# Expert rows added by DMA onto one residual row per token, instead of two stored rows per token that are combined at the end

## The chip, the cores and the metric

The kernel runs on one core of one Trainium2 chip. The metric is the device time of one execution in microseconds (us), the median of three runs. TensorE (PE) multiplies matrices, VectorE (DVE), ScalarE (ACT) and GpSimd (POOL) work on rows, SyncE (SP) only issues transfers, and 16 DMA engines carry out the transfers of all queues.

## The reference

One layer of a streaming encoder on 64 sample tokens, 16 meta tokens and 1024 prompt tokens (1104 tokens of 1024 float32 each), then a final RMSNorm. The part that the change touches is the mixture of experts: each token goes to two of 32 experts, and the two outputs, each times its gate, are added to the residual row.

```python
h = x + mix.astype(x.dtype)                       # residual row of the token
hn = rmsnorm(h, norm_ffn)
gates = p_g * top_v / sum(top_v)                  # two gates per token
expert(x) = (silu(x @ w_eg[e]) * (x @ w_eu[e])) @ w_ed[e]
h = h + gate_0 * expert_0(hn) + gate_1 * expert_1(hn)
y = rmsnorm(h, norm_final)                        # meta rows dropped
```

## The kernel before, in words

Nothing is scheduled by a planner: each engine has its own program, written out in order, and the engines meet at semaphores. A wait holds up everything behind it on its engine.

**Front stage** (to about 500 us). 1152 rows (1104 tokens and 48 padding rows) are worked in 9 tiles of 128 rows. For each tile PE projects, mixes and multiplies by the output weights; DVE adds the result to the residual tile `h_all[:, j, :]` in `back_h` (semaphore `h_added`), which stays in SBUF to the end. ACT normalises the tile and stores it to DRAM as `hn_rows`, **twice**: once in the rows of pick 0 and once in those of pick 1 (L624). The router gives each row two experts and two gates (`gate_all`, `back_weights`), and `back_rank` its place among the 96 slots of an expert. `mark` (L1332) is a small product on PE which turns one-hot matrices into the table `idx_i`: slot by expert, the row of `hn_rows`. An empty slot holds an index out of bounds, and the DMA skips it.

**Expert stage** (about 502 to 1053 us). The experts come one after another, in pairs of buffers b = 0, 1. For expert e POOL gathers up to 96 rows (`gather`, L481), PE transposes them, multiplies by the gate weights (L1412), by the up weights (L1412 again, semaphore `pe_u2`) and by the down weights (L1423, L1429, semaphore `pe_d`). DVE and ACT make the SiLU between. ACT copies the result from PSUM to `ye[b]` (L697, L699), and POOL scatters `ye[b]` to DRAM (`scatter`, L492). Each of the 2208 picks has a row of its own in `pick_rows`, so no scatter meets another. SP loads the weights, 3 x 2 MB per expert: `w_eg` (L394) as soon as the gate product of expert e-2 has freed the buffer, `w_eu` (L399) after its up product, `w_ed` (L402) after its down product.

**Extra slots.** An expert with more than 96 rows would get further blocks, in code that is there and was not entered with these inputs (n_x = 0).

**Last stage** (1053 us to the end). SP waits for the last scatters and loads `pick_rows` back, two tiles y1 and y2 for each of the 9 token tiles (L438, 18 DMAs). For each tile DVE does two operations in `combine` (L1142: y1*gate0 + h; L1144: + y2*gate1), ACT takes the sum of squares and the reciprocal root (L729 to L731), DVE normalises (L1150), and SP stores the tile (L442, L444).

Of the kernel before, what the change touches and what calls it, by code (L numbers as in the profile page):

```python
# [21 lines left out]
F32 = mybir.dt.float32  # L22
# [6 lines left out]
P = 128  # L29
# [35 lines left out]
PICK_ROWS = PICKS * TILES * P  # L65
# [17 lines left out]
           ("iota_block", BLOCK), ("iota_e", NE), ("first_g", GROUPS), ("first_e", PER_GROUP), ("pick", PICKS),  # L83
# [9 lines left out]
def constants():  # L93
# [16 lines left out]
    put("pick", p + TILES * P * np.arange(PICKS)[None, :] - NO_ROW)  # L110
# [45 lines left out]
def build(nc, x_all, state_pool, state_gla, norm_mix, w_in, w_gate_up, b_gate, w_pool, pool_scale, gla_norm, w_out,  # L156
          norm_ffn, w_router, b_router, w_eg, w_eu, w_ed, norm_final, const,
          y_prompt, y_sample, pool_prompt, gla_prompt, pool_sample, gla_sample):
    hn_dram = nc.dram_tensor("hn_rows", (PICK_ROWS, D), F32, kind="Internal").ap()
    y_dram = nc.dram_tensor("pick_rows", (PICK_ROWS, D), F32, kind="Internal").ap()  # L160

    with ExitStack() as ctx:
# [93 lines left out]
        M_tok = sb("M_tok", [P, PICKS, NE])  # L256
# [5 lines left out]
        token = sb("token", [P, PICKS])  # L262
# [4 lines left out]
        idx_f = sb("idx_f", [BLOCK, NE])  # L267
# [30 lines left out]
        idx_xf = sb("idx_xf", [BLOCK, EXTRA])  # L298
# [6 lines left out]
        def lot(n):  # L305
            return arena[:, n * D:(n + 1) * D]
        y1 = [lot(2 * i) for i in range(TILES)]
        y2 = [lot(2 * i + 1) for i in range(TILES)]
# [4 lines left out]
            w_out_in w_out_scaled hn_stored  # L313
            pe_xT pe_z pe_gate pe_qk pe_u pe_r pe_v pe_pool pe_kT pe_scores pe_kv pe_o pe_ones pe_wout pe_hT
            pe_router pe_rank pe_idx pe_hist_T pe_small_T
# [4 lines left out]
            u_kept s_sample_ready pool_out_ready outs_stored idx_ready slots_ready  # L320
            parted dve_front dve_back dve_back_o dve_rank dve_once dve_moe dve_fin act_front act_back act_once act_fin history_kept pool_steps
            pe_eT pe_g pe_u2 pe_d sig_ready hid_ready eT_ready ye_ready row_idx_ready
            x_tab_dve x_tab_pe x_idx_ready x_w x_rows x_pe x_dve x_act x_stored x_pool pick_idx_ready
            fin_ready frstd_ready g_fin_in""").split()
# [15 lines left out]
        TABLE_STEPS = 10  # L340
# [6 lines left out]
        def _(sp):  # L347
# [85 lines left out]
            for b in range(2):  # L433
                sp.wait_ge(ye_stored[b], 16 * (NE // 2))
            for i in range(TILES):
                for k, y in ((0, y1[i]), (1, y2[i])):
                    at_row = (k * TILES + i) * P
                    sp.dma_start(y[0:OUT_ROWS[i], :], y_dram[at_row:at_row + OUT_ROWS[i], :]).then_inc(y_in[i], 16)  # L438
            for i in range(TILES):
                sp.wait_ge(out_ready[i], 1)  # L440
                if i == 0:
                    sp.dma_start(y_sample, y2[i][0:SAMPLE, :]).then_inc(s["outs_stored"], 16)  # L442
                else:
                    sp.dma_start(y_prompt[(i - 1) * P:i * P, :], y2[i]).then_inc(s["outs_stored"], 16)  # L444
# [4 lines left out]
        def _(pool):  # L449
# [25 lines left out]
            pool.wait_ge(s["hn_stored"], 16 * PICKS * TILES)  # L475

            def gather(t, b):
# [4 lines left out]
                                             bounds_check=PICK_ROWS - 1, oob_is_err=False).then_inc(rows_in[b], 16)  # L482
# [17 lines left out]
            gather(1, 1)  # L500
            scatter(0, 0, first=True)
# [13 lines left out]
            pool.wait_ge(s["pe_eT"], NE)  # L515
            with pool.If(n_x > 0):
                with pool.Fori(0, EXTRA) as n:
                    with pool.If(n < n_x):
# [3 lines left out]
                                                     bounds_check=PICK_ROWS - 1, oob_is_err=False).then_inc(s["x_rows"], 16)  # L522
# [212 lines left out]
        def _(dve):  # L735
# [204 lines left out]
            def body(i, first=False, last=False, second=False, third=False):  # L940
# [6 lines left out]
                if ranking:  # L947
                    rank.begin(i - 2)
                    back_rank(i - 2, third)
# [586 lines left out]
```

## Time and profile before

| | us |
|---|---|
| median of 3 runs (1103.26 to 1104.48) | 1104.26 |
| the profiled execution | 1103.76 |
| its span, first to last instruction | 1101.9 |
| PE busy | 1012.4 (92%) |
| DVE / ACT / POOL busy | 417.4 / 240.8 / 104.8 |
| granted TensorE clock, mean | 0.966 |

The page cuts the span into 40 slices of 27.5 us. Its row PE is at 9 from the second slice to the 38th with one dip at the change of stages, and its row DMA is at 9 only in the expert stage and at the start. The last two slices hold no product. In the rows below a start is counted in us from the start of the span. SPq and POOLq are DMAs issued by that engine. "DMA to landing" is the time from the issue of a DMA to the completion of its data.

### The profile page before, as it was taken

How to read it: one execution, taken by the hardware profiler on the slowest of the kernel's cores; microseconds unless marked ns; L12 is line 12 of the kernel's file. 1: busy time of each engine (PE TensorE's matmuls, PEld its weight loads, DVE VectorE, ACT ScalarE, POOL GpSimd, SP SyncE). 2: the span in 40 equal slices, each digit the busy share in tenths (PEclk: the TensorE clock that was granted, in tenths of full speed). 3: DMA queues.
4: the chain of work that ended last, by engine and by line, in shares of the span. 5: the costliest groups of instructions: out<-in, count | busy, mean ns of one | idle time of the engine just before them, and what ended most of it. 6: DMA issues, size and time to landing. Idle time of an engine off the chain costs nothing.

```text
span 1101.9 us, 32850 instructions
## 1 busy us (share of the span) xinstructions
PE 1012.4 (92%) x14634; PEld 822.7 (75%) x14634; DVE 417.4 (38%) x909; ACT 240.8 (22%) x506; POOL 104.8 (10%) x172
## 2 busy tenths in 40 slices
PE   5999999999999999875999999999999999999920
PEld 5786777768685958435888898898888888988910
DVE  1434443535253535243432332332322323323338
ACT  2352232323332321210111111011111111111123
POOL 0110101010110101001111011011110110110000
PEclk9999999999999999986999999999999999999965
DMA  8900000000000000384999999999999999999557
GB/s 272 402 5 39 1 39 0 38 0 38 4 34 38 0 38 1 152 322 173 373 375 393 405 399 411 408 404 401 398 410 403 395 409 404 397 405 401 215 214 300
DMA packets 50850, 262.17 MB, mean 238 GB/s; under 512 B 8205, under 2 KB 10701, under 8 KB 42618
## 3 DMA queue, kind: packets, MB, share of 16 engines
q1 hardware_dynamic: 41050, 234.05, 53.8%
q0 software_dynamic: 7168, 18.10, 4.8%
q10 hardware_dynamic: 2592, 9.44, 2.1%
q8 instruction: 31, 0.51, 0.2%
q14 instruction: 9, 0.07, 0.0%
HBM read 241.84 MB, written 26.80 MB: 244 GB/s over the span
## 4 chain that ended last, share of the span: by engine, by line
PE 91%; DVE 5%; DMA 2%; issue 1%; ACT 1%; SPq 0%; ACTq 0%; DVEq 0%; POOLq 0%; POOL 0%
PE bank L1412 31%; PE bank L1178 18%; PE bank L1303 11%; PE bank L1423 10%; PE bank L1230 6%; PE bank L1429 5%; PE bank L1166 4%; DVE arena L1144 1%; DVE arena L1142 1%; PE bank L1279 1%; DMA arena<-in_w_in 1%; DVE arena L1150 1%; PE bank L1237 1%; PE bank L1296 1%; PE bank L1290 1%
## 5 line engine op out<-in xcount | busy, mean ns | idle before, releaser
L1178 PE MATMUL bank<-xnT,arena 128*128 128x128 f32 x1728 | 201.5, 278 | 4.9 <-DMA arena<-in_w_in 3.5
L1178 PEld LDWEIGHTS bank<-xnT,arena 128*128 128x128 f32 x1728 | 197.1, 193 | 7.6 <-DMA arena<-in_w_in 4.0
L1412 PEld LDWEIGHTS bank<-xnT,arena 128*64 128x64 f32 x4096 | 171.8, 138 | 8.9 <-issue 8.9
L1412 PE MATMUL bank<-xnT,arena 128*64 128x96 f32 x4096 | 175.0, 248 | 2.2 <-issue 2.2
L1412 PEld LDWEIGHTS bank<-hnT,arena 128*64 128x64 f32 x4096 | 169.6, 137 | 7.4 <-issue 7.4
L1412 PE MATMUL bank<-hnT,arena 128*64 128x96 f32 x4096 | 172.8, 246 | 0.6 <-issue 0.6
L1026 DVE TENSOR_SCALAR mixT<-mixT 128x384 f32<-128x384 f32 x32 | 11.5, 360 | 324.0 <-ACT mixT L692 324.0
L1303 PE MATMUL bank<-arena,mixT 128*128 128x512 f32 x288 | 127.8, 602 | 3.0 <-DVE mixT L859 3.0
L1303 PEld LDWEIGHTS bank<-arena,mixT 128*128 128x128 f32 x288 | 54.9, 193 | 69.4 <-issue 65.7
L1423 PE MATMUL bank<-arena,silu_r 128*32 128x384 f32 x768 | 86.0, 487 | 0.5 <-issue 0.5
L1429 PE MATMUL bank<-arena,silu_r 128*32 128x256 f32 x384 | 85.9, 380 | 0.0
L1429 PE MATMUL bank<-arena,osq 128*32 128x256 f32 x384 | 85.9, 380 | 0.0
L1423 PE MATMUL bank<-arena,osq 128*32 128x384 f32 x768 | 85.8, 488 | 0.0
L1027 DVE RECIPROCAL mixT<-mixT 128x384 f32<-128x384 f32 x32 | 81.7, 2553 | 1.1
L1230 PE MATMUL bank<-arena,xnT 128*128 128x512 f32 x144 | 64.6, 592 | 0.0
L1429 PEld LDWEIGHTS bank<-arena,osq 128*32 128x32 f32 x384 | 40.9, 110 | 15.0
L697 ACT ACTIVATE hs<-bank 96x384 f32<-96x384 f32 x32 | 13.8, 482 | 174.3 <-PE bank L1429 174.3
L697 ACT ACTIVATE kz_v<-bank 96x384 f32<-96x384 f32 x32 | 13.8, 482 | 173.5 <-PE bank L1429 173.5
L1429 PEld LDWEIGHTS bank<-arena,silu_r 128*32 128x32 f32 x384 | 40.9, 110 | 14.4
L460 POOL TENSOR_TENSOR window_work<-window_work 128x568 f32<-128x568 f32 x9 | 10.2, 1132 | 401.4 <-ACT window_work L586 401.4
L1230 PEld LDWEIGHTS bank<-arena,xnT 128*128 128x128 f32 x144 | 26.1, 190 | 26.3 <-issue 26.3
L692 ACT ACTIVATE mixT<-bank 128x384 f32<-128x384 f32 x32 | 15.7, 490 | 127.0 <-PE bank L1412 127.0
(193 smaller groups left out, 934.8 us busy)
## 6 DMA issues: line engine op xcount, KB each, us to landing
arena<-in_w_eg SPq DMA_DIRECT2D x32, 2048.0 KB
arena<-in_w_eu SPq DMA_DIRECT2D x32, 2048.0 KB
arena<-in_w_ed SPq DMA_DIRECT2D x32, 2048.0 KB, 15.4
hn_rows<-hs ACTq DMA_DIRECT2D x18, 512.0 KB, 3.5
arena<-pick_rows SPq DMA_DIRECT2D x16, 512.0 KB, 10.1
arena<-in_w_in SPq DMA_DIRECT2D x3, 2048.0 KB, 14.5
arena<-in_w_out SPq DMA_DIRECT2D x1, 4096.0 KB, 25.7
out_y_prompt<-arena SPq DMA_DIRECT2D x8, 512.0 KB, 3.5
```

The source lines that it names most:

```text
L692: A(sig[:, 0:NH], bank[2 + b][:, 0:NH], ACT.Exp, scale=-1.0).then_inc(s["sig_ready"], 1)
L697: A(ye[b][:, half * OWN:(half + 1) * OWN], bank[6 + half][0:BLOCK, 0:OWN], ACT.Copy).then_inc(s["ye_ready"], 1)
L1026: moe.then(V.tensor_scalar(gs[:, 0:NH], sig[:, 0:NH], 1.0, None, ALU.add))
L1027: moe.then(V.reciprocal(gs[:, 0:NH], gs[:, 0:NH]))
L1142: final.then(V.scalar_tensor_tensor(out=y1[i][0:r, :], in0=y1[i][0:r, :], scalar=gate_all[0:r, i, 0:1], in1=h_all[0:r, i, :], op0=ALU.mult ...
L1166: return nc.tensor.transpose(out, src, ident[0:n, 0:n])
L1178: last = mm(out, w_in_sb[:, k, a:b], xnT[:, k, :], start=k == 0, stop=k == KD - 1)
L1230: last = mm(bank[6][:, :], xnT[:, k, :], w_in_sb[:, k, V0:R0], start=k == 0, stop=k == KD - 1)
L1303: done = mm(bank[n][:, :], mixT[:, k, :], w_out_sb[:, k, n * 512:(n + 1) * 512], start=k == 0, stop=k == KD - 1)
L1412: last = mm(out[q * SW:(q + 1) * SW, n * BLOCK:(n + 1) * BLOCK], w[:, k, m * P + q * SW:m * P + (q + 1) * SW], rowsT[b][:, k, :], start=k ...
L1423: last = mm(bank[6 + half][g * TG:(g + 1) * TG, 0:OWN], tokens(k, g), wd[b][:, k, half * OWN:(half + 1) * OWN], start=k == 0, stop=k == KF ...
L1429: return mm(bank[n][TGS * TG:P, c:c + REST], tokens(k, g), wd[b][:, k, 2 * OWN:D], start=k == 0 and c == 0, stop=k == KF - 1, skip_group_c ...
```

## The change

1. `hn_rows` has one row per token, and ACT stores each normalised tile once.
2. A new DRAM tensor `sum_rows` has one row per token. SP stores each tile of the residual there as soon as it is added (`store_h`): eight before the first expert weights are loaded, the ninth behind the weights of experts 0 and 1.
3. The front stage builds, next to the table of indices, a table `gate_of_slot`: slot by expert, the gate. `mark` has 64 columns in place of 32, DVE gets `mark_gates`, and `back_weights` moves ahead of `back_rank`. For the last tile the gate half is done by PE inside expert 0, between its gate and its up product.
4. ACT multiplies by the gate while it copies the result from PSUM (`scale=gate` in `put_rows`).
5. The scatter adds (`compute_op=ALU.add`) onto `sum_rows`. As two experts may meet in one row, each scatter now waits until the one before has landed, and the first one for all residual tiles.
6. The last stage loads one row per token, 9 DMAs in place of 18, into `h_all`. `combine` is gone: ACT takes the squares of what was loaded, DVE normalises it.

```diff
-    hn_dram = nc.dram_tensor("hn_rows", (PICK_ROWS, D), F32, kind="Internal").ap()
-    y_dram = nc.dram_tensor("pick_rows", (PICK_ROWS, D), F32, kind="Internal").ap()
+    hn_dram = nc.dram_tensor("hn_rows", (ROWS, D), F32, kind="Internal").ap()
+    sum_dram = nc.dram_tensor("sum_rows", (ROWS, D), F32, kind="Internal").ap()
...
+            def store_h(j):
+                sp.wait_ge(s["h_added"], j + 1)
+                sp.dma_start(sum_dram[j * P:(j + 1) * P, :], h_all[:, j, :]).then_inc(s["h_stored"], 16)
+
+            for j in range(TILES - 1):
+                store_h(j)
             sp.wait_ge(s["pe_v"], TILES)
             load_weights(0, 0)
             load_weights(0, 1)
+            store_h(TILES - 1)
...
+            sp.wait_ge(s["h_stored"], 16 * TILES)
             for i in range(TILES):
-                for k, y in ((0, y1[i]), (1, y2[i])):
-                    at_row = (k * TILES + i) * P
-                    sp.dma_start(y[0:OUT_ROWS[i], :], y_dram[at_row:at_row + OUT_ROWS[i], :]).then_inc(y_in[i], 16)
+                sp.dma_start(h_all[0:OUT_ROWS[i], i, :], sum_dram[i * P:i * P + OUT_ROWS[i], :]).then_inc(y_in[i], 16)
...
             def scatter(t, b, first=False):
                 e = 2 * t + b
+                if not (first and b == 0):
+                    wait_parted(pool, ye_stored[1 - b], 16 * (t + b), s["parted"])
...
-                nc.gpsimd.indirect_dma_start(y_dram, bass.IndirectOffsetOnAxis(ap=pick_idx[b][:, :], axis=0), ye[b], None,
-                                             bounds_check=PICK_ROWS - 1, oob_is_err=False).then_inc(ye_stored[b], 16)
+                nc.gpsimd.indirect_dma_start(sum_dram, bass.IndirectOffsetOnAxis(ap=pick_idx[b][:, :], axis=0), ye[b], None, compute_op=ALU.add,
+                                             bounds_check=ROWS - 1, oob_is_err=False).then_inc(ye_stored[b], 16)
...
-                for k in range(PICKS):
-                    act.dma_start(hn_dram[bass.ds(k * TILES * P + j * P, P), :], hs[:, :, :].rearrange("p k n -> p (k n)")).then_inc(s["hn_stored"], 16)
+                act.dma_start(hn_dram[bass.ds(j * P, P), :], hs[:, :, :].rearrange("p k n -> p (k n)")).then_inc(s["hn_stored"], 16)
...
+            def put_rows(out, gate, step):
+                for half in range(2):
+                    A(out[:, half * OWN:(half + 1) * OWN], bank[6 + half][0:BLOCK, 0:OWN], ACT.Copy, scale=gate[:, :]).then_inc(step, 1)
...
-                act.wait_ge(s["fin_ready"], i + 1)
+                act.wait_ge(y_in[i], 16)
...
+            def mark_gates(j):
+                gates = gate_all[:, bass.ds(j, 1), :].rearrange("p a k -> p (a k)")
+                Mk = M[:, :, :, :].rearrange("p k g e -> p k (g e)")
+                return V.tensor_tensor(M_tab[:, :, NE:], Mk, gates.unsqueeze(2).to_broadcast([P, PICKS, NE]), ALU.mult)
...
-            for i in range(TILES):
-                combine(i)
-                if i:
-                    normalize(i - 1)
-            normalize(TILES - 1)
+            for i in range(TILES):
+                normalize(i)
...
+                if isinstance(t, int) and e == 0:
+                    pe.wait_ge(s["gmarks_ready"], 1)
+                    mark(NE, 2 * NE).then_inc(s["pe_gates"], 1)
                 pe.wait_ge(u_in[b], 16 * t + 16)
```

**The order on POOL** in the loop over the experts, for buffer 0: `rows_idx` and `pick_idx` hold the indices of the gather and of the scatter. Before:

```order
L481 DMA window_work<-hn_rows,rows_idx 96x1024 [waits row_idx_ready]
L121 ISA
L489 ISA [waits ye_stored0]
L489 COPY pick_idx<-idx_i 96x1
L121 REGISTER_ALU
L121 REGISTER_ALU [waits pick_idx_ready]
L492 DMA pick_rows<-kz_v,pick_idx 2304x1024 [waits ye_ready]
```

And with the change:

```order
L490 DMA window_work<-hn_rows,rows_idx 96x1024 [waits row_idx_ready]
L121 ISA
L500 ISA [waits ye_stored1,ye_stored0]
L500 COPY pick_idx<-idx_i 96x1
L121 REGISTER_ALU
L121 REGISTER_ALU [waits pick_idx_ready]
L503 DMA sum_rows<-kz_v,pick_idx 1152x1024 [waits ye_ready]
```

The wait for the other buffer's scatter is new; the next gather stands behind it.

**The order on DVE** in the last stage (first tile has 64 rows, the others 128; `fss` is the reciprocal root). Before, the first eight of 26 rows (27 operations):

```order
L1142 SCALAR_TENSOR_TENSOR arena<-arena,gate_all,h_all 64x1024
L1144 SCALAR_TENSOR_TENSOR arena<-arena,gate_all 64x1024
L1142 SCALAR_TENSOR_TENSOR arena<-arena,gate_all,h_all 128x1024
L1144 SCALAR_TENSOR_TENSOR arena<-arena,gate_all 128x1024
L1150 SCALAR_TENSOR_TENSOR arena<-arena,fss 64x1024
L1142 SCALAR_TENSOR_TENSOR arena<-arena,gate_all,h_all 128x1024
L1144 SCALAR_TENSOR_TENSOR arena<-arena,gate_all 128x1024
L1150 SCALAR_TENSOR_TENSOR arena<-arena,fss 128x1024
```

And with the change, the whole stage:

```order
L1172 SCALAR_TENSOR_TENSOR arena<-h_all,fss,arena 64x1024
L1172 SCALAR_TENSOR_TENSOR arena<-h_all,fss,arena 128x1024 x8
```

Eighteen of 27 operations are gone, and what is left waits for ACT, which waits for the load.

## Rows read from the trace of the kernel before

**Rows 1.** The page's 40 slices of the span, tenths of busy time and GB/s.
```profile
PE   5999999999999999875999999999999999999920
DMA  8900000000000000384999999999999999999557
GB/s 272 402 5 39 1 39 0 38 0 38 4 34 38 0 38 1 152 322 173 373 375 393 405 399 411 408 404 401 398 410 403 395 409 404 397 405 401 215 214 300
```

**Rows 2.** Expert stage: busy PE, PEld, DVE, ACT, POOL, clock, DMA share, GB/s.
```profile
660.00:760.00 100.00, 100.00 (x2001) 87.44 (x2001) 30.69 (x42) 14.91 (x36) 14.19 (x24) 1.00 1.02 405
```

**Rows 3.** Timeline of SP: last two loads of down weights (start, duration).
```profile
1002.82 0.38 SPq L402 DMA_DIRECT2D arena<-in_w_ed  x1
...
1019.66 0.38 SPq L402 DMA_DIRECT2D arena<-in_w_ed  x1
```

**Rows 4.** Line L402, landing of its 5 loads issued from 500 to 600 us.
```profile
DMA to landing us min/median/max: 10.8/12.5/14.9
```

**Rows 5.** Line L402, landing of the load issued at 1002.82 us.
```profile
DMA to landing us min/median/max: 18.1/18.1/18.1
```

**Rows 6.** Timeline of PE: first down products of experts 30 and 31.
```profile
1030.92 0.52 PE L1423 MATMUL bank<-arena,osq 128*32 128x384 f32 x3
...
1047.52 0.52 PE L1423 MATMUL bank<-arena,silu_r 128*32 128x384 f32 x3 [0.51 <-issue]
```

**Rows 7.** The page's DMA queues: packets, MB, share of 16 engines' span.
```profile
q1 hardware_dynamic: 41050, 234.05, 53.8%
q0 software_dynamic: 7168, 18.10, 4.8%
```

**Rows 8.** Timeline of POOL: the scatters of experts 28 and 31, the last one.
```profile
1005.79 0.94 POOL L492 DMA_INDIRECT pick_rows<-kz_v,pick_idx  x1 [13.76 <-ACT kz_v L699]
...
1055.86 0.92 POOL L492 DMA_INDIRECT pick_rows<-hs,pick_idx  x1 [15.38 <-ACT hs L699]
```

**Rows 9.** Line L492, all 32 scatters.
```profile
DMA to landing us min/median/max: 3.3/7.1/9.5
```

**Rows 10.** Groups of the last stage by form: busy, mean ns, idle before.
```profile
L1144 DVE SCALAR_TENSOR_TENSOR arena<-arena,gate_all 128x1024 f32<-128x1024 f32 x8 | 10.3, 1285 | 0.3
L1150 DVE SCALAR_TENSOR_TENSOR arena<-arena,fss 128x1024 f32<-128x1024 f32 x8 | 10.2, 1280 | 0.6 <-ACT fss L731 0.6
L1142 DVE SCALAR_TENSOR_TENSOR arena<-arena,gate_all,h_all 128x1024 f32<-128x1024 f32 x8 | 10.2, 1277 | 0.0
L729 ACT ACTIVATE arena<-arena 128x1024 f32<-128x1024 f32 x8 | 8.5, 1057 | 14.8 <-DVE arena L1144 14.8
L730 ACT ACTIVATE fss<-fss,eps 128x1 f32<-128x1 f32 x8 | 2.4, 294 | 0.3
L731 ACT ACTIVATE fss<-fss 128x1 f32<-128x1 f32 x8 | 1.6, 203 | 0.3
L729 ACT ACTIVATION_READ_ACCUMULATOR arena<-arena 128x1 f32 x8 | 1.5, 186 | 0.0
```

**Rows 11.** Timeline of the last stage: SP's loads, DVE's first and last operation.
```profile
1059.23 11.49 SPq L438 DMA_DIRECT2D arena<-pick_rows  x18
1064.68 1.28 DVE L1142 SCALAR_TENSOR_TENSOR arena<-arena,gate_all,h_all 64x1024 f32<-64x1024 f32 x1 [16.02 <-DMA arena<-pick_rows]
...
1097.55 1.28 DVE L1150 SCALAR_TENSOR_TENSOR arena<-arena,fss 128x1024 f32<-128x1024 f32 x1 [0.58 <-ACT fss L731]
```

**Rows 12.** Line L438, landing of the 18 loads.
```profile
DMA to landing us min/median/max: 4.1/9.4/15.1
```

**Rows 13.** Line L444, landing of the 8 stores of the output.
```profile
DMA to landing us min/median/max: 2.6/3.5/11.9
```

**Rows 14.** A stretch of the last stage, columns as in rows 2.
```profile
1065.00:1080.00 15.00, 0.00 (x0) 0.00 (x0) 14.82 (x13) 6.59 (x16) 0.00 (x0) 0.50 1.03 412
```

**Rows 15.** Timeline of a front tile: DVE's wait before the ranks, PE's `mark`.
```profile
267.57 0.19 DVE L921 TENSOR_TENSOR R<-bank,counts 128x32 f32<-128x32 f32 x1 [2.02 <-PE bank L1327]
...
274.61 0.45 PE L1332 MATMUL bank<-M_tok,at_rank 128*96 128x32 f32 x4
```

More of the change, by code:

```diff
@@ L306, in lot @@
             return arena[:, n * D:(n + 1) * D]
-        y1 = [lot(2 * i) for i in range(TILES)]
-        y2 = [lot(2 * i + 1) for i in range(TILES)]
+        squares = [lot(2 * i) for i in range(TILES)]
+        y_out = [lot(2 * i + 1) for i in range(TILES)]
         g_fin = lot(2 * TILES)
@@ L515, in _ @@
             pool.wait_ge(s["pe_eT"], NE)
+            for b in range(2):
+                pool.wait_ge(ye_stored[b], 16 * (NE // 2))
             with pool.If(n_x > 0):
@@ L684, in _ @@
             back_router(TILES - 1)
+            def put_rows(out, gate, step):
+                for half in range(2):
+                    A(out[:, half * OWN:(half + 1) * OWN], bank[6 + half][0:BLOCK, 0:OWN], ACT.Copy, scale=gate[:, :]).then_inc(step, 1)
+                for g, (n, c) in enumerate(REST_AT):
+                    own = slice(g * TG, (g + 1) * TG)
+                    A(out[own, 2 * OWN:D], bank[n][BLOCK:P, c:c + REST], ACT.Copy, scale=gate[own, :]).then_inc(step, 1)
             def expert(t, b, first=False):
@@ L695, in expert @@
                     act.wait_ge(ye_stored[b], 16 * t)
-                for half in range(2):
-                    A(ye[b][:, half * OWN:(half + 1) * OWN], bank[6 + half][0:BLOCK, 0:OWN], ACT.Copy).then_inc(s["ye_ready"], 1)
-                for g, (n, c) in enumerate(REST_AT):
-                    A(ye[b][g * TG:(g + 1) * TG, 2 * OWN:D], bank[n][BLOCK:P, c:c + REST], ACT.Copy).then_inc(s["ye_ready"], 1)
-            act.wait_ge(s["hn_stored"], 16 * PICKS * TILES)
+                if first and b == 0:
+                    act.wait_ge(s["gates_ready"], 1)
+                put_rows(ye[b], gate_of_slot[:, bass.ds(e, 1)], s["ye_ready"])
+            act.wait_ge(s["hn_stored"], 16 * TILES)
             expert(0, 0, True)
@@ L932, in back_rank @@
                     rank(V.tensor_scalar(at_rank[:, k, :], con("iota_block"), rk[:, k:k + 1], None, ALU.is_equal))
-                V.tensor_tensor(M_tok[:, :, :], Mk, token[:, :].unsqueeze(2).to_broadcast([P, PICKS, NE]), ALU.mult).then_inc(s["onehot_ready"], 1)
+                if not last:
+                    rank(mark_gates(j))
+                V.tensor_scalar(M_tab[:, :, 0:NE], Mk, token[:, 0:1], None, ALU.mult).then_inc(s["onehot_ready"], 1)
             def back_idx(j):
@@ L948, in body @@
                     rank.begin(i - 2)
+                    back_weights(i - 2)
                     back_rank(i - 2, third)
@@ L992, in _ @@
             rank.begin(j - 1)
+            back_weights(j - 1)
             back_rank(j - 1)
@@ L1004, in _ @@
             rank.begin(j)
-            back_rank(j)
+            back_rank(j, last=True)
             dve.wait_ge(s["idx_added"], TILES)
             dve.wait_ge(s["pe_idx"], TILES)
-            V.tensor_tensor(idx_i[:, :], idx_f[:, :], bank[7][0:BLOCK, 192:192 + NE], ALU.add).then_inc(s["idx_ready"], 1)
+            V.tensor_tensor(idx_i[:, :], idx_f, bank[7][0:BLOCK, 192:192 + NE], ALU.add).then_inc(s["idx_ready"], 1)
             back_weights(j)
+            mark_gates(j).then_inc(s["gmarks_ready"], 1)
             moe = Steps(dve, s["dve_moe"])
@@ L1391, in _ @@
             ranks(j)
-            mark(j)
+            pe.wait_ge(s["onehot_ready"], j + 1)
+            mark(0, NE).then_inc(s["pe_idx"], 1)
             STRIPS = 2
@@ L1452, in expert @@
                 pe.wait_ge(s["hid_ready"], 2 * e + 2)
-                if not (isinstance(t, int) and e == 0):
+                if isinstance(t, int) and e == 0:
+                    pe.wait_ge(s["gates_ready"], 1)
+                else:
                     pe.wait_ge(s["ye_ready"], YE_STEPS * e)
```

111 lines of the change are left out of this document (54 added, 57 removed).

## The prediction

> **What bounds the kernel now.** I read the 40 slices first [rows 1]. The reader is to see that PE is at 9 almost from start to end, that DMA is at 9 only in the expert stage, and that two slices at the end hold no product at all. Then I took one stretch of the expert stage [rows 2]: in 100 us PE is busy for 100.00 and the DMA share is 1.02 at 405 GB/s. So two resources are full at once, at a granted clock of 1.00, the higher of its two levels (2.4 GHz). PE sets the pace, one expert in 1019.66 - 1002.82 = 16.84 us [rows 3]. Per expert the DMA engines move 6.29 MB of weights (32 such sets), and 2208/32 = 69 picked rows of 4096 B in and again out, 0.57 MB: 6.86 MB in 16.84 us are 407 GB/s, the 405 of the row.
>
> That the DMA engines have nothing to spare shows in the landing of the down weights. The first ones take 10.8 to 14.9 us [rows 4], one near the end 18.1 us [rows 5]: a queue that grows under a constant demand. It does no harm yet. The weights of expert 30 land at 1002.82 + 18.1 = 1020.9 and are used at 1030.9, so 10.0 us are left; for expert 31 the use is at 1047.5 [rows 3, 5, 6]. These 10 us are the only cover that the change has for more DMA work.
>
> The last stage is bound by DVE: 27 operations back to back from 1064.68 to 1098.8 [rows 11], 1.28 us each [rows 10], with almost no idle time before them, while ACT waited 14.8 us for them. After DVE's last operation 3 us remain for the last store [rows 13] (2.6 at least), and the span ends at 1101.9.
>
> **The last stage.** Eighteen operations of `combine` go, 10.3 + 10.2 us for 16 of them [rows 10] and 2.6 for the first tile's two. What is late next? Three chains have to be worked out from the issue of the last scatter, 1055.86 [rows 8]. It landed in at least 3.3 us [rows 9], which gives the loads' issue at 1059.23 [rows 11]. An add has to read its target first; I give it 1 us more, so the loads are issued at 1060.2.
> - ACT: the first tile lands 4.1 us later [rows 12], at 1064.3. ACT takes 1.057 + 0.186 + 0.294 + 0.203 = 1.74 us per tile [rows 10], nine tiles 15.7: 1080.0. DVE's 1.28 and a store of 2.6 to 3.5 follow [rows 10, 13]: 1084.
> - DMA: 4.46 MB in and 4.46 MB out at 412 GB/s [rows 14] are 21.7 us. They start about 1.5 us after the issue and need about 1.5 us to complete the last: 1085.
> - DVE: nine operations of 1.28, hidden behind ACT.
>
> The loads go first in the same queue, so the stores can't start before them, and DMA is the bound: the end is at 1085 in place of 1101.9, **16.9 us earlier**. The DMA bytes of this stage fall from 13.4 to 8.9 MB.
>
> **The expert stage.** Scatters stay 32, with the same 69 rows each, but each row is now read from DRAM, added and written. The trace has no adding DMA. From below it costs nothing more: if the read of the target passes beside the writes of other rows. Less than nothing is excluded, as the same rows are still read from SBUF and written to DRAM. From above, if each row had to finish before the next could start, 69/16 = 4.3 rows per engine would each hold it for a large part of the 3.3 us of the fastest scatter [rows 9], say 2.4: 10 us per expert. Between them lie two rows. The loads' queue q1 took 53.8% of 1101.9 us for 234.05 MB, which is 0.166 us of one engine per 4096 B; q0, with gathers and scatters, 4.8% for 18.10 MB, 0.192 us per row with its overhead [rows 7]. One more read of 4096 B, at the rate of q1, is 4.3 x 0.166 = **0.72 us per expert**; as costly as a whole second row of q0 it would be 0.83. I take 0.72, as the added part is a read without a descriptor for a new row; the row nearest to it is q1's.
>
> What of it is paid: when the weights of expert 30 are needed, scatters 0 to 28 have been issued (28 at 1005.79 [rows 8]). 29 x 0.72 = 20.8 us of DMA work, less the 10.0 us left: PE waits **10.8 us** in total, in the second half of the experts. With the queue already full the waits come first where 0.72 x e passes the time left, after about 17 experts. For expert 31 it is 30 x 0.72 - 10 or a little less, so the one before decides.
>
> A page of the Trainium skill bears on this: Collectives: The Full Stack, section The bandwidth ceiling. It says that a reduction in the DMA engines is slow by its two source reads on one ring and not by the sum, with a measured ratio of 1.93 to a copy. No run here shows it yet. By that rule the extra would be 0.93 x 0.192 x 4.3 = 0.77 us per expert, 12.3 us of waits and a time 1.5 us over my forecast: an estimate from the page's ratio.
>
> **The small parts.** `hn_rows` is stored once: 9 x 0.5 MB less, in the front stage, where DMA is mostly idle (1 to 39 GB/s in its slices [rows 1]), so nothing is won; `store_h` puts 9 x 0.5 MB back there, hidden by the same idle time. The ninth stands behind the weights of expert 1 and replaces in amount the second store of the last `hn_rows` tile: zero. If that cover were gone each would cost 0.5 MB/405 GB/s = 1.3 us. SP's early waits for `h_added` are over before it would load the first expert weights, so they hold up nothing. On DVE `mark_gates` adds some 0.2 us per tile and `back_weights` comes earlier; both fall into DVE's idle 2.02 us before the ranks [rows 15]. On PE `mark` doubles its columns: 0.45 us with 32 [rows 15], at most doubled in each of 8 tiles and once more in expert 0, but the fixed part is most of it; I take 0.6 us for all, between 0 and 4. ACT's scale comes with the copy, 15% busy [rows 2]: nothing. The new wait on POOL for the previous scatter: it lands after 7.1 us [rows 9], the next is issued 16.84 us later, so even twice the landing time costs nothing. Behind it stands the next gather.
>
> **Sum.** -16.9 + 10.8 + 0.6 = -5.5. The profiled execution took 1103.76, so 1098.3. That execution is 0.5 below the median shown, within the spread of 1103.26 to 1104.48.
>
> **The rivals.**
> - *The read is hidden.* Engines are seen busy by packets, not by bytes on each side, and an add may use the idle read side of a write. Then the 10 us of cover stay and the time is 1103.76 - 16.9 + 0.6 = 1087.5. For it: reads and writes are two directions. Against: gathers and scatters, in opposite directions, add up to a share of 1.02, so they do not pass beside each other. All costs up to 10.0/29 = 0.34 us per expert end here.
> - *The add holds an engine longer (the other side).* Place: the same rows of the scatter; price: each microsecond per expert above the cover is paid 29 times. The change wins nothing from (16.9 - 0.6 + 10.0)/29 = 0.91 us per expert on, only a quarter above my value. With two more packet times per row, 0.33 us, it is 1.43 us per expert: 41.5 - 10.0 = 31.5 us of waits, 1119. For it: three accesses in place of two, the sum itself, and engines that differ in speed, of which the slowest decides. Against: no row. One row at a time would end far outside, near 1380.
> - *The gain is given back just so.* 0.83 to 0.98 us per expert gives 1101.5 to 1106, no change.
> - *The chained scatters.* If an adding scatter landed after more than 16.84 us, POOL would fall behind by the rest in every expert and the gathers with it; 18 us would cost 1.2 x 30 = 35 us, 1123. Against: 7.1 us now [rows 9].
>
> **Chances.** Main case (0.34 to 0.83 us per expert) 0.37; read hidden 0.18; no change 0.12; slower by a longer hold 0.29; by the chain 0.04. What a measurement can tell from no change is 0.2%, 2.2 us. So faster 0.55, same 0.12, slower 0.33. The main case alone reaches from 1088 to 1101.5. The range of 8 in 10 has the hidden read at its lower end and the longer hold at its upper: 1086.5 to 1128.
>
> **What would show it.** In the profile after, the share of q0 tells the price of the add: 4.8% now, about 6.9% by my value, 9% with two packet times. PE's waits for arena<-in_w_eg, in_w_eu or in_w_ed should appear after expert 17 and sum to some 11 us, with the landing of `w_ed` grown to 28 us. The last stage should take 29 us from the issue of the last scatter to the end, in place of 46. I am wrong if the landing stays below 20 us (the read is hidden), if waits begin before expert 10 (a longer hold), if PE's clock falls under 1.00 in the expert stage because of the waits, or if the last stage keeps over 35 us.

## The result, and the profile after

The kernel after takes 1106.47 us (median of 20 runs, 1101.09 to 1112.19) against 1103.24 for the kernel before in the same comparison. The ratio is 1.0028, with a 95% interval of 1.0016 to 1.004: **slower by 0.3%**, where I forecast 1098.3, faster by 0.5%. The profiled execution has a span of 1104.8 us, 2.9 more than before.

The change trades two stages. The best mark between them is the issue of the last scatter. The timeline of the kernel after (start, duration, engine, operation) shows it, and the last stage behind it:

```profile
510.96 1.39 PE L1434 MATMUL bank<-xnT,arena 128*64 128x96 f32 x14 [1.16 <-issue]
...
1074.93 1.42 POOL L503 DMA_INDIRECT sum_rows<-hs,pick_idx  x1 [9.62 <-ACT hs L706]
1079.29 4.45 SPq L447 DMA_DIRECT2D h_all<-sum_rows  x9
1083.33 1.06 ACT L747 ACTIVATE arena<-h_all 64x1024 f32<-64x1024 f32 x1 [9.24 <-DMA h_all<-sum_rows]
...
1097.89 1.28 DVE L1172 SCALAR_TENSOR_TENSOR arena<-h_all,fss,arena 128x1024 f32<-128x1024 f32 x1 [0.32 <-ACT fss L749]
```

From the last scatter to the end it is now 1104.8 - 1074.93 = 29.9 us, in place of 1101.9 - 1055.86 = 46.0 [rows 8]: 16.2 us won. But the last scatter is issued 1074.93 - 1055.86 = 19.1 us later. 1.4 us of these were there before the first gate product (510.96, in place of 509.57 in the trace before), 17.7 arose in the expert stage. The line of the trace before:

```profile
509.57 2.79 PE L1412 MATMUL bank<-xnT,arena 128*64 128x96 f32 x31 [1.16 <-issue]
```

The page's slices of the kernel after, against [rows 1], show where:

```profile
PE   5999999999999999875999999999999999999970
DMA  8900000000000000384999999999999999999948
GB/s 270 403 4 39 1 39 0 38 7 31 19 19 38 0 38 1 152 315 171 367 355 387 389 389 397 381 388 376 382 380 374 391 371 385 378 388 375 392 170 328
```

The row PE hides the loss (a 9 is anything above 90%); the row GB/s tells it: some 380 in place of 400 in the expert stage. Windows of the kernel after, columns as in [rows 2]:

```profile
660.00:760.00 100.00, 100.00 (x1996) 87.31 (x1994) 30.42 (x43) 17.67 (x36) 17.44 (x24) 1.00 1.02 386
760.00:860.00 100.00, 96.70 (x1911) 83.80 (x1908) 29.74 (x41) 17.18 (x35) 15.43 (x22) 1.00 1.02 379
860.00:960.00 100.00, 93.86 (x1883) 82.45 (x1883) 30.89 (x42) 15.22 (x31) 16.09 (x23) 1.00 1.02 383
960.00:1053.00 93.00, 87.67 (x1725) 75.83 (x1721) 26.63 (x36) 14.72 (x30) 13.18 (x19) 1.00 1.02 382
```

The DMA share is the same 1.02 as before while the bytes per second fell: the engines are as busy and move less. PE is at 100.00 in the first of these windows and falls short by 3 to 6 us in each later one, at an unchanged clock of 1.00. PE's waits after 760 us say for what (total, times, longest):

```profile
PE bank L1434 <- DMA arena<-in_w_eg: 8.0, 11, 1.3
PE bank L1445 <- DMA arena<-in_w_ed: 6.6, 8, 1.3
```

The first of these waits is not at 760 us but at 820.27, before the gate product of expert 18. The timeline shows it, with the issue of the down weights just before it and of the last ones:

```profile
820.27 10.78 PE L1434 MATMUL bank<-xnT,arena 128*64 128x96 f32 x256 [0.73 <-DMA arena<-in_w_eg]
```
```profile
819.73 0.38 SPq L405 DMA_DIRECT2D arena<-in_w_ed  x1
...
1037.73 0.38 SPq L405 DMA_DIRECT2D arena<-in_w_ed  x1
```

Each such issue follows the down product of one expert. From 600.82 to 819.73 they come every 16.84 us, as before. The next twelve experts take (1037.73 - 819.73)/12 = 18.17 us each: **once PE waits, an expert costs 1.33 us more**, 15.9 of the 17.7 us.

The DMA queues, against [rows 7]:

```profile
q1 hardware_dynamic: 41114, 234.31, 54.4%
q0 software_dynamic: 7168, 18.10, 6.8%
```

q0, with the scatters, took 6.8% of 1104.8 = 75.1 us of 16 engines, before 4.8% of 1101.9 = 52.9: 22.2 us more, **0.69 us per expert**, where I had put 0.72. But q1, which carries the weights, took 601.0 us in place of 592.8 for nearly the same bytes. This term of 8.2 us, on average 0.26 per expert, is in no line of my sum.

The landing of the down weights (line L405), issued between 500 and 600 us and between 820 and 860 us, to set beside [rows 4, 5]:

```profile
DMA to landing us min/median/max: 9.3/14.1/15.7
...
DMA to landing us min/median/max: 30.3/30.6/30.7
```

It starts as before and grows to 30.6 us, all the time that there is between issue and use. From then on PE waits.

### The profile page after: what moved, and what is told of

The parts are those of the page before. It is cut to its first block, busy times and chain, and to the rows that moved or that the text cites. A ratio compares the mean times of both kernels' runs of the same rounds, so it can differ in the third digit from the quotient of the medians.

```text
span 1104.8 us, 32980 instructions
## 1 busy us (share of the span) xinstructions
PE 1016.2 (92%) x14638; PEld 824.2 (75%) x14638; DVE 393.9 (36%) x903; ACT 254.7 (23%) x506; POOL 121.5 (11%) x172
## 3 DMA queue, kind: packets, MB, share of 16 engines
q1 hardware_dynamic: 41114, 234.31, 54.4%
## 4 chain that ended last, share of the span: by engine, by line
PE 73%; DMA 21%; DVE 2%; ACT 2%; issue 1%; SPq 0%; ACTq 0%; DVEq 0%; POOLq 0%; POOL 0%
PE bank L1434 21%; DMA arena<-in_w_eg 19%; PE bank L1197 18%; PE bank L1322 11%; PE bank L1445 6%; PE bank L1249 6%; PE bank L1451 3%; PE bank L1185 3%; PE bank L1298 1%; DMA arena<-in_w_in 1%; ACT arena L747 1%; PE bank L1315 1%; PE bank L1256 1%; PE bank L1309 1%; PE bank L1340 0%
## 5 line engine op out<-in xcount | busy, mean ns | idle before, releaser
L1249 PE MATMUL bank<-arena,xnT 128*128 128x512 f32 x144 | 64.6, 592 | 0.0
L703 ACT ACTIVATE kz_v<-bank,tab_f 96x384 f32<-96x384 f32 x32 | 16.7, 572 | 183.7 <-PE bank L1451 183.7
L703 ACT ACTIVATE hs<-bank,tab_f 96x384 f32<-96x384 f32 x32 | 16.7, 572 | 176.9 <-PE bank L1451 176.9
L1451 PEld LDWEIGHTS bank<-arena,osq 128*32 128x32 f32 x384 | 40.9, 110 | 15.0
L1445 PEld LDWEIGHTS bank<-arena,osq 128*32 128x32 f32 x768 | 30.5, 110 | 16.7 <-issue 7.3
## 6 DMA issues: line engine op xcount, KB each, us to landing
arena<-in_w_in SPq DMA_DIRECT2D x3, 2048.0 KB, 14.6
```

What stands on the lines that cost most here:

```text
L703: A(out[:, half * OWN:(half + 1) * OWN], bank[6 + half][0:BLOCK, 0:OWN], ACT.Copy, scale=gate[:, :]).then_inc(step, 1)
L1249: last = mm(bank[6][:, :], xnT[:, k, :], w_in_sb[:, k, V0:R0], start=k == 0, stop=k == KD - 1)
L1445: last = mm(bank[6 + half][g * TG:(g + 1) * TG, 0:OWN], tokens(k, g), wd[b][:, k, half * OWN:(half + 1) * OWN], start=k == 0, stop=k == KF ...
L1451: return mm(bank[n][TGS * TG:P, c:c + REST], tokens(k, g), wd[b][:, k, 2 * OWN:D], start=k == 0 and c == 0, stop=k == KF - 1, skip_group_c ...
```

## The experiments

All times are medians beside the kernel before on the same chip (1102.8 to 1104.2). "Plain scatter" is the changed kernel without the add, so that the rows overwrite the residual and each other: it measures, and computes something else.

**1. The add alone taken away.**

```diff
-  nc.gpsimd.indirect_dma_start(sum_dram, ..., ye[b], None, compute_op=ALU.add,
+  nc.gpsimd.indirect_dma_start(sum_dram, ..., ye[b], None,
```

> The changed kernel with a plain scatter: the rows overwrite the residual rows in DRAM instead of being added (the sum of the experts is left out). The chain of scatters, the gate scaling on ACT, the stores of the residual and the short last stage stay. Theory A (the add occupies the DMA engines): the share of q0 falls from 6.8% to 4.8%, the landing of the down weights stays under 20 us, PE waits for no weights, and the 17.1 us that the expert stage grew by go: about 1089.5. Theory B (the waits come from the chained scatters or the slower copies on ACT, not from the add): PE still waits and the time stays near 1106.

Measured 1087.13 (ratio 0.9852, 0.9831 to 0.9874). The add costs 19.3 us, everything else together won 15.7. Of this kernel: its queues, a window, the landing of expert 30's down weights (issued at 1002.63) and their first use:

```profile
q1 hardware_dynamic: 41114, 234.31, 54.9%
q0 software_dynamic: 7168, 18.10, 4.9%
```
```profile
660.00:760.00 100.00, 100.00 (x2005) 87.43 (x2004) 30.87 (x41) 17.64 (x36) 13.67 (x23) 1.00 1.02 404
```
```profile
DMA to landing us min/median/max: 21.6/21.6/21.6
```
```profile
1030.80 0.52 PE L1445 MATMUL bank<-arena,osq 128*32 128x384 f32 x3
```

No product waits for weights. The cover left for expert 30 is 1030.80 - 1002.63 - 21.6 = 6.6 us in this trace, less than the 10.0 that I read in the trace before.

**2. The add in the first 16 experts, or in the last 16.** The second kernel is the first with the two halves changed over.

```diff
+  how = {'compute_op': ALU.add} if add else {}      # add: experts 0 to 15
...
-  ... ye[b], None, compute_op=ALU.add,
+  ... ye[b], None, **how,
```

> The changed kernel, but only the scatters of experts 0 to 15 add, those of 16 to 31 are plain (their sums are left out). Theory A with a cover that is used up first: the add costs 0.93 us of DMA work per expert (0.69 on q0 and 0.24 on the weights' queue), 16 of them 14.9 us, less the 10 us of cover: 5 us of waits, about 1094.5. Theory C (each add costs PE its share at once, with no cover): half of 17.1 us, about 1098.

> Only the scatters of experts 16 to 31 add, those of 0 to 15 are plain (rows shared with these keep one of the two). The twin of the run in which the first 16 add (1096.6, that is 9.4 more than all plain). Theory D (the cover is small, about 2 us, and every microsecond of added work above it is paid later): 16 x 0.69 = 11, less the last two whose weights have landed, less 2: 7.5 to 9 us more than all plain, 1095 to 1096, with no wait before 780 us. Theory G (cover of 10 us as I predicted): 14 x 0.69 - 10 = 0, 1087 to 1089.

First half 1096.57 (0.9931, 0.9909 to 0.9954), last half 1091.48 (0.9893, 0.987 to 0.9915): 8.7 and 4.5 us over the plain scatter by their ratios. The first lies between its two theories (1094.5 and 1098). The windows with the add in the first half:

```profile
660.00:760.00 100.00, 100.00 (x2009) 87.61 (x2002) 30.86 (x41) 17.64 (x36) 17.40 (x24) 1.00 1.02 382
760.00:860.00 100.00, 96.76 (x1911) 83.84 (x1911) 27.41 (x39) 17.64 (x36) 15.04 (x24) 1.00 1.02 388
860.00:960.00 100.00, 96.66 (x1900) 83.52 (x1897) 31.32 (x42) 16.20 (x33) 11.69 (x21) 1.00 1.02 393
```

While the adds run, nobody waits: the last one is issued at 786.09, PE's first wait is at 795.19. So theory C, a price paid at once, is out: the adds build up a debt of DMA work, and PE pays when the landing has reached the time of use. 13.2 us for the two halves against 19.3 for the whole: part of each half's debt was covered. The last half came out lower than I expected (7.5 to 9), between the two theories.

There is more in these two traces than a debt that is paid once. With the add in the first half, the down weights are issued at

```profile
782.75 0.38 SPq L405 DMA_DIRECT2D arena<-in_w_ed  x1
...
1028.71 0.38 SPq L405 DMA_DIRECT2D arena<-in_w_ed  x1
```

so fourteen experts with plain scatters took 17.57 us each, 0.73 above the pace, to the end; with plain scatters from the start none did. Queue q1 from 820 to 1000 us, with the add in the first half and then in the last:

```profile
q1 hardware_dynamic: 8552, 65.47, 92.9%
```
```profile
q1 hardware_dynamic: 8216, 63.60, 88.6%
```

That is 2.55 us of the 16 engines per MB (92.9% of 180 us over 65.47 MB) with plain scatters behind a debt, and 2.51 with adds before any wait. In the same stretch the five kernels in which PE waits for most of the time (these first-half adds, the kernel after, its versions of experiments 5 (expert 2) and 7, shape d of experiment 6) have 2.55 to 2.57, and the five without waits there (before, its chained version, both plain ones, last-half adds) 2.47 to 2.51. **The weights' transfers are slower where the backlog is deep, not where the adds are.**

**3. More reading in the indirect queue.** Plain scatter, and a second gather of the same rows into unused SBUF.

```diff
+  nc.gpsimd.indirect_dma_start(h_all[0:BLOCK, TILES - 1 - b, :], None, hn_dram, bass.IndirectOffsetOnAxis(ap=pick_idx[b][:, :], axis=0), ...)
```

> The plain scatter of the first experiment, and after each scatter one more indirect gather of the same numbers of rows (from hn_rows into SBUF, never used): the read that an add needs, as a DMA of its own. Its price by the rate of q0 before is 69/16 x 0.192 = 0.83 us per expert. Theory A1 (only the packets' own time counts): 29 x 0.83 - 10 = 14 us of waits, about 1103.5, q0 at 7.2%. Theory A2 (any additional traffic also slows the weights' packets, by 0.24 us per expert as the add did): 21 us of waits, about 1110.5.

Measured 1151.74 (1.0433, 1.0374 to 1.0493), far above both: 64.6 us for the gather. Its queues:

```profile
q1 hardware_dynamic: 41114, 234.31, 54.9%
q0 software_dynamic: 10752, 27.15, 7.3%
```

Of a span of 1147.2 us, q0 takes 30.6 us more than with one gather, and q1 630 in place of 596: **the transfers of the weights, unchanged, take 34 us longer**. My accounts had no such term at all. Not all of the 64.6 us are waits for weights: from 565 to 759 us, before the first of these, eleven experts took 17.61 us each, 0.77 above the pace. The profile names no cause for that.

**4. The chain of scatters in the kernel before.**

```diff
+  if not (first and b == 0):
+      wait_parted(pool, ye_stored[1 - b], 16 * (t + b), s["parted"])
```

> The kernel before with one edit: each scatter waits until the previous one has landed, as in the changed kernel. Theory A: it lands after 7 to 10 us and the next is issued 16.8 us later, so no change, 1103.2, ratio within 0.2% of 1. Theory B: POOL falls behind and the time grows by some us.

1102.9, ratio 1.0003 (0.999 to 1.0016). The chain is free; the landing in the kernel after, 10.8 us in the median (11.7 at most), is below the 17 us of an expert.

**5. The same work moved out of the expert stage, at two places.** The residual tiles are in DRAM now, so their 32 KB per partition can hold the gate and up weights of one expert, 4.2 MB, loaded in the front stage. First for expert 2, then for expert 18. Nothing is left out.

```diff
+  def load_ahead(n, w, name):      # n: 0 gate, 1 up; e = 2, or 18
+      sp.wait_ge(s["h_stored"], 16 * (4 * n + 4))
+      sp.wait_ge(s["hs_ready"], 4 * n + 4)
+      sp.dma_start(ahead[n], w[e * D:(e + 1) * D, :].rearrange("(p k) n -> p k n", k=KD)).then_inc(s[name], 16)
...
```

> The changed kernel, all scatters adding, with the gate and up weights of expert 2 (4.2 MB, 10.4 us at 404 GB/s) loaded during the front stage into the residual tiles that have already gone to DRAM. This work leaves the expert stage, in which the DMA engines are the bound. Theory D (the waits of PE are DMA work above what the stage can hold): waits fall by about 10 us, 1106.5 - 10.4 = 1096, faster than both kernels. Theory H (the waits come from packets that are slower or uneven whenever adds are under way, not from the total): gain below 5 us, 1102 or more. If the early loads disturb the front stage the time is higher than either by what the front stage grows (0.5 MB to 4 MB in slices that hold 1 to 39 GB/s: not expected).

> The changed kernel, all scatters adding, with the gate and up weights of expert 18 (in place of expert 2) loaded in the front stage into the residual tiles. The same 4.2 MB leave the expert stage, but at a place where the transfers' queue is at its deepest (landing of the down weights 30 us). Theory C (cover can't be stored before the buffers are full: for expert 2 the engines just fell idle, and only where there is a backlog does leaving out 4.2 MB count): the landing falls by some 10 us at expert 18 and the waits by 9 to 10 us, 1097. Theory H (the waits come from something that a shorter queue does not mend): 1104 or more, as with expert 2.

For expert 2: 1107.9 (1.0032, 1.0013 to 1.0051), nothing won, where theory D had 1096. For expert 18: 1093.79 (0.9912, 0.9893 to 0.993), 13 us below the kernel after, 3 us more than theory C gave. The landing of the down weights issued between 820 and 860 us in the two kernels, expert 2's first:

```profile
DMA to landing us min/median/max: 30.9/30.9/30.9
```
```profile
DMA to landing us min/median/max: 19.4/19.5/19.6
```

And the window in which the early weights of expert 2 are not loaded (its DMA share is 0.73, in the kernel after 0.79):

```profile
460.00:560.00 100.00, 77.51 (x1220) 60.03 (x1223) 43.65 (x135) 13.62 (x30) 9.39 (x14) 0.85 0.73 273
```

A lead can't be stored at the start: each buffer is refilled only when the expert two before has freed it, and engines without a request fall idle (273 in place of 291 GB/s in this window, 1.8 of the 4.2 MB; the rest is argued). At expert 18, where the queue is deep, the same 4.2 MB lower the landing by 11 us.

**6. The same bytes in three shapes.** Plain scatter, and one extra plain load of 295 kB per expert, issued by SP behind the down weights. A fourth kernel has shape a twice.

```diff
+  sp.dma_start(h_all[0:72, 7, :],     hn_dram[0:72, :])      # a: 72 rows of 4096 B
+  sp.dma_start(h_all[0:96, 7, 0:768], hn_dram[0:96, 0:768])  # b: 96 rows of 3072 B
+  sp.dma_start(h_all[:, 7, 0:576],    hn_dram[0:P, 0:576])   # d: 128 rows of 2304 B
```

> The scatters are plain (rows that two experts share keep only one of them), and SP issues behind each expert's down weights one more plain load of 72 rows of 4096 B from hn_rows into SBUF, which nobody uses. It is 72/16 x 0.166 = 0.75 us of the 16 engines per expert, nearly the same as what the add was measured to take in its own queue (0.69). The plain scatter alone measured 1087.1. Theory D (what the add costs is DMA work, whatever its kind, and the 10 us left before the weights are needed are not worth 10 us): as the add, 19.3 x 0.75/0.69 = 21 us more, 1108. Theory E (the rest of the add's cost is special to adding in DRAM, and plain work is paid only above the 10 us): 29 x 0.75 - 10 = 12 us more, 1099. Theory F (extra work of the indirect queue is what is dear, as the extra gather suggests): below 1099.

> As the kernel with one extra plain load per expert, but with two of them, 1.5 us of the 16 engines per expert; scatters are plain (shared rows keep one expert). The difference to the run with one load is the slope once the cover is gone. Pure work: 31 x 0.75 = 23 us more than with one load. Theory D: 1108 + 23 = 1131, or more if a deep queue slows every packet. Theory E: 1099 + 22 = 1121. If the slope is far above 0.75 us per expert, the weights' own packets become slower with a deeper queue, as in the run with the extra gather (1151.7).

> As the kernel with plain scatters and one extra plain load of 295 kB per expert (1176.3), with the same bytes from the same place laid out as 128 rows of 2304 B in place of 72 rows of 4096 B. By the number of its small completion packets (12 per load in place of 16) the load of 72 rows went to 12 of the 16 engines only; 128 rows go to all 16. The scatters are plain (shared rows keep one expert). Theory S (uneven engines): nearly all of the 89 us go, what stays is about 0.75 us per expert above the cover, 1087.1 + 12 to 22 = 1099 to 1109. Theory R (reading the same rows of DRAM again and again, or extra reads as such, slow all packets): still above 1150.

> As the kernels with plain scatters and one extra plain load of 295 kB per expert, the same bytes from the same place laid out as 96 rows of 3072 B: all 16 engines carry it, six partitions of SBUF each as with the gathers and scatters, in place of eight as with the weights. 72 rows of 4096 B on 12 engines gave 1176.3, 128 rows of 2304 B on 16 engines 1107.9. Theory S (what slows the weights' packets is that the engines drift apart, which here they do not): near 1107.9, within 5. Theory P (what slows them is that an engine writes to partitions that are another engine's in the transfers of the weights): clearly above, 1130 or more.

Shape a: 1176.33 (1.0655), above every theory; twice: 1258.05 (1.1415), 82 us more where pure work was 23; b: 1157.76 (1.0473, 1.0414 to 1.0532), d: 1107.88 (1.0041, 1.0026 to 1.0056). Queue q1 and a window of a, b and d, in this order:

```profile
q1 hardware_dynamic: 43718, 243.46, 57.8%
...
860.00:960.00 100.00, 85.72 (x1553) 72.27 (x1555) 20.84 (x28) 14.36 (x30) 11.54 (x20) 0.93 1.00 340
```
```profile
q1 hardware_dynamic: 44586, 243.46, 58.1%
...
860.00:960.00 100.00, 88.58 (x1684) 75.48 (x1680) 26.05 (x35) 14.70 (x30) 11.54 (x20) 0.97 1.01 361
```
```profile
q1 hardware_dynamic: 45578, 243.46, 56.5%
...
860.00:960.00 100.00, 93.13 (x1869) 81.82 (x1864) 30.70 (x41) 15.22 (x31) 13.26 (x23) 1.00 1.02 397
```

The same bytes cost 89, 71 or 21 us over the plain scatter. The packets tell the split: without the extra load there are 41114, so the 31 loads have 84, 112 and 144 each, which is 72 + 12, 96 + 16 and 128 + 16, a small packet for each engine that takes part. Shape a goes to 12 engines; b and d go to all 16, with six and with eight partitions each. As b is even and still costs 50 us more than d, uneven engines are not the main reason, and the numbers fall on the side of theory P: **a transfer that is cut among the engines in another way than the weights slows the weights' packets**. That is not shown to the end: b and d also differ in the length of a row (3072 and 2304 B), and no run has the one without the other. q1 took 56.5% of 1106.0 = 625 us in d, 29 more than without the load; in b 672, 76 more. In a and b a small part comes from PE's clock, 0.93 and 0.97 in the window, after its waits.

The Trainium skill has the rule for the split (DMA: Bandwidth & Descriptors, section Why a DMA increments its semaphore by 16 and not by 1): the number of engines is the largest up to 16 that divides the outer size, so 12 for 72. The packets here agree. The same page (section The descriptor swizzle) says that in a transfer to 128 partitions each engine writes to one SBUF port of its own; the three times fit this, but no run shows a port.

**7. The first engine turned.** A row's number within its expert decides its slot: the kernel deals the rows out in turn to 16 groups of six slots, always beginning with the same group. Counted from the reference's routing, the first group has 152 of the 2208 rows, the last 125, the mean is 138. The counters now start elsewhere for each expert (fullest group 143). I take a group to be the share of one DMA engine; the traces don't show rows by engine. Nothing is left out.

```diff
-  V.memset(counts[:, :], 0.0).then_inc(s["setup_dve"], 1)
+  for k, start in enumerate((0, 8, 4, 12)):
+      last = V.memset(counts[:, :].rearrange("p (e k) -> p e k", k=4)[:, :, k], float(start))
+  last.then_inc(s["setup_dve"], 1)
```

In the changed kernel, in that with plain scatters, and in that with a second gather:

> The changed kernel, all scatters adding, with one edit: the counters that number an expert's rows start at 0, 8, 4 or 12 (by e mod 4) in place of 0. Slot c of the index table lies in the c-th of 96 partitions, six partitions to a DMA engine, and rows are dealt out one to each engine in turn; so now the engine that gets the first row is another one for each expert. With these inputs the first engine carries 152 of the 2208 rows and the mean is 138; with the edit the most loaded one carries 143. Theory S (the slowest of the 16 engines sets the pace, and the remainder of the division by 16 always falls on the same ones): 9 rows fewer on it, each for a gather (0.185 us) and an adding scatter (about 0.34 us), so waits fall by about 5 us, 1106.5 - 5 = 1101.5, and the weights' packets get faster as the engines stay closer together. Theory M (only the mean load counts): no change, 1106.5.

> The changed kernel with plain scatters and the counters that start at 0, 8, 4 or 12. There are no waits to save, so the time stays near 1087. Theory S: the landing of the last down weights, 20.2 and 21.6 us with all counters at 0, falls by 9 x 0.37 = 3.3 us or more, to 17 or 18: the cover that was missing at the end. Theory P or mean load: it stays above 20.

> The kernel with plain scatters and one more gather per expert (1151.7), with the counters that start at 0, 8, 4 or 12. The fullest engine now has 143 rows in place of 152, three times (gather, second gather, scatter), 9 x 0.56 us = 5 us less. Theory S (drift of the engines slows the weights' packets too, which cost 33 us there): at least half of the 64 us go, 1120 or less. Theory P (partitions): only the 5 us of the rows go, 1145 to 1148.

The changed kernel with it: 1101.99 (0.9987, 0.9975 to 0.9999), 4.5 us less, as theory S had it. In its trace PE's first wait comes two experts later (851.33), and behind it an expert still costs 1.34 us more. With plain scatters: 1088.2 in a single run, and its last two down weights landed after (line L405, issued from 1000 to 1040 us; it was 20.2 and 21.6):

```profile
DMA to landing us min/median/max: 15.1/15.8/16.5
```

So the uneven shares seem to have eaten cover: it is about 12 us where they are even, by one trace of each. With a second gather: 1140.42 (1.0356, 1.0315 to 1.0396), 11 us less, 8.5 by the ratios, whose intervals overlap. That is far from half, so theory S fails there; whether it is more than the 5 us of the rows isn't shown, the less so as this kernel ran at 16.84 us per expert in the stretch where experiment 3 ran at 17.61. q1 still took 55.2% of 1137.6 = 628 us there, so the slow weights' packets are not cured by even shares.

**8. Both edits together** (expert 18 ahead, counters turned).

> The changed kernel with both edits: the counters that start at 0, 8, 4 or 12, and the gate and up weights of expert 18 loaded ahead. If both reasons are right the waits of 15 us are nearly gone: 1087.1 (plain scatters, no waits) + 0 to 5, so 1088 to 1093, faster than both kernels. If only the one about the backlog is right 1097, if only the one about uneven engines 1101.5.

1090.52 (0.9883, 0.9861 to 0.9904): 1.2% below the kernel before and 1.4% below the kernel after, by the ratios. It computes everything. Its window and waits:

```profile
860.00:960.00 100.00, 100.00 (x1998) 87.33 (x1995) 30.60 (x41) 17.65 (x36) 17.42 (x24) 1.00 1.02 380
```
```profile
PE bank L1455 <- DMA arena<-in_w_eg: 2.4, 4, 0.7
...
PE bank L1466 <- DMA arena<-in_w_ed: 1.6, 2, 1.1
```

## Why the prediction was wrong

**Last stage, -16.9: right.** 16.2 us were won, and 29.9 us stayed where I had said 29; the last add was followed by the loads after 4.4 us, as I had put it. I had named DMA as the bound, 1 us behind ACT's chain. ACT's chain led up to the last DVE operation (DVE waits 0.32 us for the tile), and from its end, 1099.17, the last store took 5.6 us where I had 2.6 to 3.5, so both had a part. In [rows 1] one digit was read too strictly: the 39th slice still holds products (2 tenths), only the last has none. Nothing in the sum hangs on it.

**Price of the add in its own queue, 0.72 us per expert: right** (0.69). The estimate by the rule of the Trainium skill that I had weighed (Collectives: The Full Stack, The bandwidth ceiling), 0.77 by its ratio, is 12% above what was measured, my row 4%.

**The expert stage's waits, +10.8: the step that failed.** The stage grew by 17.7 us, of which PE's waits for weights are 8.0 + 6.6 = 14.6. The form of the sum was right: DMA work above PE's pace, less a cover, paid in the second half of the experts. The first wait comes with expert 18, where I had said after 17. What failed is the line "29 x 0.72 = 20.8 us of DMA work, less the 10.0 us left", as it prices an expert behind the cover at 0.72 us like one before it. Measured there: 1.33 us, in twelve experts.
- 0.69 us of it are the add's own packets, as the line has it.
- The unchanged transfers of the weights became slower, which the line leaves out: in the stretch from 820 to 1000 us 2.56 us per MB in place of 2.50, some 0.37 us per expert of 6.29 MB. On average over the run it is 0.26, and 29 x (0.69 + 0.26) - 10.0 = 17.6 gives the measured growth. The adds themselves don't seem to cause it: of the 8.2 us of q1, 3.1 are there with plain scatters too (595.9 against 592.8), and experiment 2 has the slow transfers where no add runs any more. Experiments 3 and 6 show how large such an effect can be: 34 us with an extra gather, and up to 50 between two shapes of the same bytes.
- The rest of the 1.33, some 0.27 us, stays open.

The line also used the mean over 16 engines, although I had written that "the slowest decides". To even out the shares gave 4.5 us back, by a later first wait and not by a lower price behind it. This overlaps with the other parts, so it must not be added to them.

**The cover of 10.0 us** was read well enough for the trace before, but it is no constant of the kernel: 6.6 us with plain scatters and about 12 with even shares, by one trace of each. By 6.6 the add's 19.3 us come out nearly: q0's and q1's growth between the plain scatter and the kernel after is 21.9 + 5.1 us, 29/32 of it less 6.6 is 17.9. That two such averages come close is a consistency, not a proof of either cover.

**Small parts, +0.6.** The start of the expert stage is 1.4 us later in these two traces, inside the bound of 0 to 4. The chained scatters cost nothing, as said.

**The rivals.** "The read is hidden" fell with q0's 6.8%. "The add holds an engine longer" has the right sign and the wrong mechanism: it wanted 9% in q0. The break-even that I had worked out, 0.91 us per expert, fits the result: the average of 0.69 + 0.26 = 0.95 lies just above it. The case "given back just so" (1101.5 to 1106) missed by 0.5 us.

What stays open: why the weights' transfers are slower in a deep backlog. That an engine which leaves its own partitions slows the others is no more than suggested by the shapes of experiment 6; the same shape with another row length, and a gather or scatter laid out in eight partitions to an engine, were not tried. Why the cover is 6.6 us with plain scatters and 10.0 before, at equal shares, isn't known.

## What to carry to other kernels

Where PE and the DMA engines are both full, as here, a DMA edit can have three prices: its own packets, the slowing of the other packets, and its share on the fullest of the 16 engines (argued here from experiment 7, not seen by engine); look at GB/s under a constant DMA share, since a fall there holds the second price. Work out the price of a unit behind the cover by itself: here it was 1.33 us per expert, nearly twice the edit's own packets, and in experiment 2 a price of 0.73 went on after the adds had stopped. A debt in the transfers' queue shows as a landing time that grows long before anyone waits, and work is best taken out where the landing is longest, not at the start where it only makes engines idle. When rows are dealt out in turn, start the deal elsewhere each time, and try for each small transfer the shape that the big ones have.

## What the runs showed of the hardware

- One extra load of 295 kB per expert cost 21 us over the run as 128 rows of 2304 B, 71 as 96 rows of 3072 B and 89 as 72 rows of 4096 B, although longer rows make fewer packets.
- In the stretch from 820 to 1000 us q1 took 2.55 to 2.57 us of the 16 engines per MB in the five kernels in which PE waited in most of it, and 2.47 to 2.51 in the five in which it didn't, whether the scatters added or not.
- An adding scatter occupies POOL for 1.45 us where a plain one takes 0.94 [rows 8], and lands in 10.8 us in the median in place of 7.1 [rows 9]. Its own packets cost (75.1 - 53.2) x 16/2208 = 0.16 us per row more than those of the plain scatter.
- PE's granted clock stayed at 1.00, the higher of its two levels (2.4 GHz), in the windows of the kernel after, with waits of up to 1.3 us. In a window of shape a the mean was 0.93, where single waits were up to 2.9 us in the run.
